# Seven block products in place of eight for one pair of weight pieces per group, in the last network's down projections

## The chip, the cores and the metric

The kernel runs on one core of a Trainium2 chip. The metric is the device time of one execution in microseconds (us), the median of several. The engines are PE (TensorE matmul), PEld (its weight loads), DVE (VectorE), ACT (ScalarE), POOL (GpSimd) and SP (SyncE, which only issues transfers here).

## The reference, cut to what matters

Two transformer blocks run one after the other on 256 tokens of width 2048, all in fp32. The change touches only the end of the second block, its feed-forward network:

```python
hn = rms_norm_2(h, norm_ffn_g)
gate, up = jnp.split(hn @ w_gate_up, 2, axis=-1)     # 2048 -> 2 x 5632
h = h + (jax.nn.silu(gate) * up) @ w_down            # 5632 -> 2048
out = rms_norm_2(h, norm_final_g)
```

## The kernel before

**Precision.** An fp32 product is made of three matmuls on rounded operands. Every operand is split in a high part and a low part (the remainder), and the kernel sums high x high, high x low and low x high. For weights ACT writes the high part (`hi`, line L552) and DVE subtracts it from the raw weights to give the low part (`lo`, L899).

**Pieces and groups.** Weights come as pieces of two k-tiles (2 x 128 rows) by 512 columns. One transfer, issued by SP, brings two pieces into one of four slots of `raw`; SP may refill a slot when both of its pieces have been split by DVE. `hi` and `lo` are rings of four pieces: ACT may write piece n when PE has used up piece n-4 (semaphore `pieces_used`). A group is the sum over some pieces into PSUM. Groups alternate between banks 0 to 3 and 4 to 7.

**The last network.** It is worked in three thirds. `f2_up0`, `f2_up1`, `f2_up2` form the hidden values of 2048, 2048 and 1536 columns, a gate group and an up group in turn, eight pieces each, 24 matmuls of 256 moving columns to a piece (L1491, L1502). After each, `f2_down0`, `f2_down1`, `f2_down2` multiply these by their part of `w_down`: four groups of 512 output columns each, of 8, 8 and 6 pieces. Here the stationary operand is a 128 x 128 tile of hidden values and the moving one is 512 columns of weights: 2 k-tiles x 2 token halves x 3 products = 12 matmuls of 512 columns to a piece (L1528 to L1530, in `piece`). Each group uses two of its four banks.

**The order on ACT and DVE.** `walk` writes it out. At piece j of a group it first calls `split` for the piece that lies AHEAD = 3 ahead (so the piece j+3 is split while PE works on j), and at the last piece it calls `evacuate` for the group. So the splits of the next group's pieces 0, 1, 2 stand in front of a group's evacuation, and that of piece 3 stands behind it (`more()` pulls a split in between steps of an evacuation). Both engines run in order.

**Evacuations.** For `f2_up` the up group's is: `work` = sums x row scale (L990), `more()`, `work` x silu (L993), ACT's copy to the high hidden values in `B` (L634), DVE's low part (L1103). For `f2_down0` and `f2_down1` (kind `tpart`): one DVE add of the two banks into `HT` (L1086). For `f2_down2` (kind `tlast`): that add, two ACT squares with sums (L608), then DVE's multiplication with the final gain (L1098). The very last group has a separate ending, in which PE takes its last four pieces twice, once for each half of the tokens (`last_pieces`), and DVE and ACT scale and store the output.

**Loops.** `f2_up1`, `f2_up2`, `f2_down0` and `f2_down1` run as hardware loops over turns (two groups to a turn); `f2_up0` and `f2_down2` are written out.

Of the kernel before, what the change touches and what calls it, by code (L numbers as in the profile page):

```python
# [25 lines left out]
P = 128  # L26
# [107 lines left out]
def ffn(add, name, n, gate, up, down, kinds, layout):  # L134

    src = n - 4
    for c, groups in enumerate((4, 4, 3)):
        first = 4 * GC * c
        add(f"{name}_up{c}", groups, ["gate", "up"], 8, ("A", "halves", src),
            [(gate[0], 0, gate[1] + first, GC), (up[0], 0, up[1] + first, GC)], peel=0 if c else groups if name == "f2" else 1)  # L140
        add(f"{name}_down{c}", 2, [kinds[c]] * 2, 2 * groups, ("B", layout, n),
            [(down, first, 0, 2 * GC), (down, first, GC, 2 * GC)], peel=2 if c == 2 else 0)
        n += groups
    return n + 4 if kinds[2] == "res_gate" else n

# [50 lines left out]
    return first or EVERY_TURN.get((seg.name, at))  # L196


class Tally:


# [35 lines left out]

def bass_two_blocks(nc, ins, out):
    SEGS, TOTAL = schedule()

    with ExitStack() as ctx:
        def sem(name):
# [5 lines left out]
        def overlay(**shapes):  # L248
# [16 lines left out]
        _, qk = overlay(pad_qk=[P, 8 * BROW], qk=[P, 16, T])  # L265
        _, xtok = overlay(pad_x=[P, 8 * BROW], xtok=[P, 2, D])
        B = sb("B", [P, KT, BROW], F32R)
        h = sb("h", [P, KT, T])
        pb_copy = sb("pb_copy", [P, MT, T])
        work = sb("work", [P, MT, T])  # L270
# [22 lines left out]
        _, win_a, win_b, win_c = overlay(g1_a=[P, KT * T], win_a=[P, MT, TM], win_b=[P, MT, TM], win_c=[P, MT, TM])  # L293
        _, cvv, cvg, cvo = overlay(g1_b=[P, KT * T], cvv=[P, MT, TV], cvg=[P, MT, TV], cvo=[P, MT, T])
        _, HT, gfin_row = overlay(silu_b=[P, MT * T], HT=[P, 2, D], gfin_row=[P, D])
        sb("arena", [P, 10368])

        ps = ctx.enter_context(nc.psum_tensor("ps", [P, 8, 512], F32))
# [23 lines left out]
        sums_written, sums_landed = sem("sums_written"), sem("sums_landed")  # L322
        skew_written, bias_landed, late_landed, stored = (
            sem("skew_written"), sem("bias_landed"), sem("late_landed"), sem("stored"))
        NTABLES = 19

        block = ctx.enter_context(nc.Block())
# [96 lines left out]
        def _(pool):  # L424
# [40 lines left out]
            small_loads(2)  # L465
            small_loads(3)

        def first_tile(seg, turn, g):
# [9 lines left out]
        def walk(eng, tallies, split, evacuate, side, each_turn, last):  # L478

            at = {"split": AHEAD}

            for seg in SEGS:
                def run(turn, t):
                    base = seg.p0 + (t or 0) * seg.per_turn

                    def split_to(end):

                        while at["split"] < end:  # L490
                            n = turn * seg.per_turn + seg.p0 + at["split"]
                            if not isinstance(n, int) or n < TOTAL:
                                split(n, base + at["split"])
                            at["split"] += 1

                    for g, kind in enumerate(seg.kinds):
                        G = turn * len(seg.kinds) + seg.g0 + g
                        for j in range(seg.pieces):
                            p = g * seg.pieces + j
                            split_to(p + 1 + AHEAD)  # L500
                            if j == seg.pieces - 1:
                                left = [MORE.get(kind, 0)]
# [6 lines left out]
                                b0 = 4 * ((seg.g0 + g + (t or 0) * len(seg.kinds)) % 2)  # L509
# [12 lines left out]
                if seg.turns > 1:  # L522
                    steady = AHEAD + MORE.get(seg.kinds[-1], 0)
                    lead = 0 if at["split"] == steady else 1
                turns_of(eng, seg, tallies, run, lead)
            last()


        @block.scalar
        def _(act):  # L530
# [12 lines left out]
            def split(n, slot):  # L543

                raw_slot = slot // 2 % RAWS
                if isinstance(n, int):
                    act.wait_ge(raw_landed[raw_slot], landed(n // 2))
                elif slot % 2 == 0 or slot < AHEAD:
                    act.wait_ge(raw_landed[raw_slot], turn_landed(n, slot))
                if not isinstance(n, int) or n >= RING:  # L550
                    act.wait_ge(pieces_used, n - RING + 1)
                act.activation(hi[:, slot % RING], raw[:, raw_slot, 2 * (slot % 2):2 * (slot % 2) + 2, :],  # L552
                               ACT.Copy).then_inc(hi_ready, 1)

            def turn_landed(n, slot):

# [317 lines left out]
            walk(act, {1: asked, 2: given, 3: ready}, split, evacuate, side, lambda quarter, turn: None, last)  # L874


        @block.vector
        def _(dve):
# [15 lines left out]
            def split(n, slot):  # L894

                dve.wait_ge(hi_ready, n + 1)
                if not isinstance(n, int) or n >= RING:
                    dve.wait_ge(pieces_used, n - RING + 1)
                dve.tensor_tensor(lo[:, slot % RING], raw[:, slot // 2 % RAWS, 2 * (slot % 2):2 * (slot % 2) + 2, :],  # L899
                                  hi[:, slot % RING], ALU.subtract).then_inc(lo_ready, 1)  # L900

            def sums_done(end):

# [526 lines left out]
            walk(dve, {0: own, 1: asked, 2: given, 3: ready}, split, evacuate, side, turn_h, last)  # L1430


        @block.tensor
        def _(pe):
# [127 lines left out]
            def side(seg, what, G):  # L1562
# [67 lines left out]
                elif isinstance(what, tuple):  # L1630
# [25 lines left out]
                    elif name == "turn_out":  # L1656
# [3 lines left out]
                                last = pe.transpose(ps[:, 6, e * T + a * P:e * T + (a + 1) * P], o_head[:, a, e * P:(e + 1) * P], ident[:, :])  # L1660
                        done.mark(last)

            def last_pieces(seg, b0):

                first = seg.pieces - RING
                for a in range(2):
                    if a == 1:
                        pe.wait_ge(residual_added, 1)
                    for j in range(first, seg.pieces):
                        n = TOTAL - seg.pieces + j  # L1670
                        if a == 0:
                            pe.wait_ge(lo_ready, n + 1)
                        for kk in range(2):
                            k = 2 * j + kk
                            Xh, Xl = (x[:, k, a * P:(a + 1) * P] for x in token_parts)
                            to = ps[:, b0 + a, :]
                            pe.matmul(to, Xh, hi[:, n % RING, kk, :], start=False, stop=False, skip_group_check=True)  # L1677
                            pe.matmul(to, Xh, lo[:, n % RING, kk, :], start=False, stop=False, skip_group_check=True)  # L1678
                            last = pe.matmul(to, Xl, hi[:, n % RING, kk, :], start=False, stop=j == seg.pieces - 1 and kk == 1, skip_group_check=True)  # L1679
                        if a == 1:  # L1680
                            last.then_inc(pieces_used, 1)
                    if a == 0:
                        last.then_inc(half_done, 1)

            for seg in SEGS:
                def run(turn, t):
                    for g, kind in enumerate(seg.kinds):
# [10 lines left out]
                        for j in range(seg.pieces - RING if at_end else seg.pieces):  # L1698
# [54 lines left out]
```

## Time and profile before

| | |
|---|---|
| median of 3 runs | 2615.46 us (2615.27 to 2615.46) |
| profiled execution, first to last instruction (span) | 2613.5 us |
| PE busy share of the span | 100% |
| DVE, ACT, POOL busy share | 62%, 45%, 1% |
| mean granted TensorE clock | 0.999 of 2.4 GHz |

The profiled execution is known by its span; the median of the runs lies 2.0 us above it, which is taken for what lies around a span. Times in the rows below are us from the start of the span unless ns is said; a matmul's busy time is longer than the distance between the starts of two, since matmuls are pipelined.

### The profile page before, as it was taken

Reading aid. Unit: us, or ns where it says so; the run is one execution under the profiler, and the core shown is the slowest. Engines: PE = TensorE matmul, PEld = TensorE weight load, DVE = VectorE, ACT = ScalarE, POOL = GpSimd, SP = SyncE. Lnnn points to the kernel's source line nnn. Section 1 sums busy time; section 2 is a strip of 40 time slices with the busy share of each in tenths; the row PEclk is TensorE's granted clock in tenths of the full one; section 3 lists DMA queues with packets and bytes.
Section 4 is the critical chain, followed back from the end, with each engine's and each line's share of the span. In section 5 each row is a group of like instructions: output and inputs, shape, how many; then the busy total and the mean of one; then the engine's idle time right before and its main releaser. Section 6 shows DMA issues by size and latency. Waiting matters only on the chain.

```text
span 2613.5 us, 50693 instructions
## 1 busy us (share of the span) xinstructions
PE 2604.7 (100%) x21336; PEld 2544.6 (97%) x21336; DVE 1614.5 (62%) x1692; ACT 1169.1 (45%) x1259; POOL 14.6 (1%) x33
## 2 busy tenths in 40 slices
PE   9999999999999999999999999999999999999998
PEld 8989999999999999999999999999999989998997
DVE  7668765555555556795676666556777655555555
ACT  5356554434443444464443333444544434443444
POOL 2000000000000000000000000000000000000000
PEclk9999999999999999999999999999999999999999
DMA  9654556565655565555555555555565555555553
GB/s 306 202 168 163 196 193 197 185 201 188 199 186 200 189 200 192 179 202 196 181 183 192 190 183 191 195 190 196 193 210 194 194 193 193 192 193 193 192 193 130
DMA packets 254438, 503.95 MB, mean 193 GB/s; under 512 B 9390, under 2 KB 11456, under 8 KB 254160
## 3 DMA queue, kind: packets, MB, share of 16 engines
q1 hardware_dynamic: 250160, 496.27, 57.2%
q10 hardware_dynamic: 3136, 4.21, 0.5%
q8 instruction: 111, 1.82, 0.3%
q0 software_dynamic: 992, 1.34, 0.2%
q14 instruction: 39, 0.32, 0.0%
HBM read 498.89 MB, written 2.89 MB: 192 GB/s over the span
## 4 chain that ended last, share of the span: by engine, by line
PE 100%; DVE 0%; ACT 0%; POOL 0%; issue 0%; DVEq 0%; POOLq 0%
PE ps L1491 49%; PE ps L1502 25%; PE ps L1528 4%; PE ps L1530 4%; PE ps L1529 4%; PE ps L1549 4%; PE ps L1558 4%; PE ps L1553 3%; PE ps L1539 1%; PE ps L1538 1%; PE ps L1536 1%; PE ps L1444 0%; PE ps L1451 0%; PE ps L1679 0%; PE ps L1678 0%; PE ps L1677 0%
## 5 line engine op out<-in xcount | busy, mean ns | idle before, releaser
L899 DVE TENSOR_TENSOR lo<-raw,hi 128x1024 fp32r<-128x1024 f32 x939 | 1142.6, 1224 | 864.5 <-ACT hi L552 850.3
L552 ACT ACTIVATE hi<-raw 128x1024 fp32r<-128x1024 f32 x939 | 990.3, 1060 | 1237.0 <-PE ps L1502 938.8
L1491 PE MATMUL ps<-A,hi 128*128 128x256 f32 x7286 | 902.8, 276 | 0.0
L1491 PEld LDWEIGHTS ps<-A,hi 128*128 128x128 f32 x7286 | 861.0, 188 | 0.3
L1491 PE MATMUL ps<-B,hi 128*128 128x256 f32 x3963 | 491.0, 276 | 0.0
L1502 PE MATMUL ps<-A,lo 128*128 128x256 f32 x3648 | 487.7, 276 | 0.0
L1491 PEld LDWEIGHTS ps<-B,hi 128*128 128x128 f32 x3963 | 468.2, 188 | 0.1
L1502 PEld LDWEIGHTS ps<-A,lo 128*128 128x128 f32 x3648 | 447.3, 188 | 0.0
L1502 PE MATMUL ps<-B,lo 128*128 128x256 f32 x1984 | 265.2, 276 | 0.0
L1502 PEld LDWEIGHTS ps<-B,lo 128*128 128x128 f32 x1984 | 243.3, 188 | 0.0
L1529 PE MATMUL ps<-lo,B 128*128 128x512 f32 x336 | 130.7, 389 | 0.0
L1528 PE MATMUL ps<-hi,B 128*128 128x512 f32 x336 | 130.7, 389 | 0.0
L1530 PE MATMUL ps<-hi,B 128*128 128x512 f32 x336 | 130.7, 389 | 0.0
L1549 PE MATMUL ps<-B,hi 128*128 128x260 f32 (+3 forms) x768 | 109.0, 284 | 0.0
L1558 PE MATMUL ps<-B,lo 128*128 128x258 f32 (+3 forms) x768 | 108.7, 284 | 0.0
L1553 PE MATMUL ps<-B,hi 128*128 128x256 f32 x768 | 104.1, 278 | 0.0
L1549 PEld LDWEIGHTS ps<-B,hi 128*128 128x128 f32 x768 | 100.0, 189 | 0.0
L1558 PEld LDWEIGHTS ps<-B,lo 128*128 128x128 f32 x768 | 98.9, 189 | 0.0
L1553 PEld LDWEIGHTS ps<-B,hi 128*128 128x128 f32 x768 | 96.3, 188 | 0.0
L1528 PEld LDWEIGHTS ps<-hi,B 128*128 128x128 f32 x336 | 63.1, 188 | 13.1
L1530 PEld LDWEIGHTS ps<-hi,B 128*128 128x128 f32 x336 | 63.1, 188 | 13.0
L1529 PEld LDWEIGHTS ps<-lo,B 128*128 128x128 f32 x336 | 63.1, 188 | 13.0
(264 smaller groups left out, 1235.0 us busy)
## 6 DMA issues: line engine op xcount, KB each, us to landing
raw<-in_w_in_dram SPq DMA_DIRECT2D x135, 1024.0 KB, 5.2
raw<-in_ffn_w_dram SPq DMA_DIRECT2D x132, 1024.0 KB, 5.1
raw<-in_w_gate_up_dram SPq DMA_DIRECT2D x88, 1024.0 KB, 5.0
raw<-in_w_down_dram SPq DMA_DIRECT2D x44, 1024.0 KB, 5.1
raw<-in_w_out_dram SPq DMA_DIRECT2D x16, 1024.0 KB, 5.1
raw<-in_pl_w_gate_dram SPq DMA_DIRECT2D x16, 1024.0 KB, 5.0
raw<-in_conv_out_w_dram SPq DMA_DIRECT2D x16, 1024.0 KB, 5.1
raw<-in_w_o_dram SPq DMA_DIRECT2D x16, 1024.0 KB, 5.0
```

Of the source, the lines that this page charges most:

```text
L552: act.activation(hi[:, slot % RING], raw[:, raw_slot, 2 * (slot % 2):2 * (slot % 2) + 2, :], ACT.Copy).then_inc(hi_ready, 1)
L899: dve.tensor_tensor(lo[:, slot % RING], raw[:, slot // 2 % RAWS, 2 * (slot % 2):2 * (slot % 2) + 2, :], hi[:, slot % RING], ALU.subtract). ...
L1491: pe.matmul(ps[:, b0 + m, 0:T], high(slot, kk, m), x, start=j == 0 and kk == 0 and part == 0, stop=False)
L1502: last = pe.matmul(ps[:, b0 + m, 0:T], low(slot, kk, m), Xh, start=False, stop=j == seg.pieces - 1 and kk == 1)
L1528: pe.matmul(to, Xh, hi[:, slot % RING, kk, :], start=first, stop=False)
L1529: pe.matmul(to, Xh, lo[:, slot % RING, kk, :], start=False, stop=False)
L1530: last = pe.matmul(to, Xl, hi[:, slot % RING, kk, :], start=False, stop=final)
L1536: pe.matmul(to, Wh, Xh, start=first and m % 2 == 0, stop=False, skip_group_check=True)
L1538: pe.matmul(to[:, a:b], Wh, Xl[:, a:b], start=False, stop=False, skip_group_check=True)
L1549: pe.matmul(ps[:, b0 + m, 0:with_lo], high(slot, kk, m), B[:, 2 * j + kk, 0:with_lo], start=first and kk == 0, stop=False, skip_group_chec ...
L1553: pe.matmul(ps[:, b0 + m, 0:T], high(slot, kk, m), B_low[:, 2 * j + kk, :], start=False, stop=False, skip_group_check=True)
L1558: last = pe.matmul(ps[:, b0 + m, 0:with_hi], low(slot, kk, m), B[:, 2 * j + kk, 0:with_hi], start=False, stop=final and kk == 1, skip_grou ...
```

## The change

For pieces 2 and 3 of every group of the three down projections but the very last group (11 pairs), the two pieces of weights and the hidden values they meet are read as 2 x 2 blocks (two k-tiles by two column halves, two token halves by two k-tiles), and the 2 x 2 block product is made with seven products of blocks and not eight, in the manner of Strassen and Winograd. `seven_products` on PE makes them: each is three matmuls of 256 columns, 42 to a pair, where 24 of 512 columns stood.

For this, POOL forms sums of weight blocks from `raw` (`block_sums`, four `tensor_tensor` of 128 x 512 elements to a pair, one of them in place in `raw`), ACT and DVE split three of these into `t_hi` and `t_lo` (128 x 1536 elements), sums of the hidden values are formed once to each third (`activation_sums`, at the up evacuation of the second turn), and `combine` adds the parts of the products that lie in two more banks into `HT`, by one ACT copy and five DVE operations, at piece 5 of the group. ACT's split of piece 2 waits for POOL, and so does DVE's of piece 3. The loops of the last network are written out.

```diff
-            ... peel=0 if c else groups if name == "f2" else 1)
+            ... peel=groups if name == "f2" else 0 if c else 1)
-            ... peel=2 if c == 2 else 0)
+            ... peel=2 if c == 2 or name == "f2" else 0)
+SEVEN_AT = 2
+SEVEN_COLS = GC // 2
+def seven_product_pairs(segs):
+    first = [x.p0 + turn * x.per_turn + g * x.pieces + SEVEN_AT
+             for x in segs if x.name.startswith("f2_down") for turn in range(2) for g in range(2)]
+    return {n: q for q, n in enumerate(first[:-1])}
...
+            def block_sums(n, q):                                    # GpSimd
+                w = raw[:, n // 2 % RAWS, :, :].rearrange("p (i e) (s c) -> p i e s c", e=2, s=2)
+                t3, t2, t4 = (t_sum[:, :, i, :] for i in range(3))
+                pool.wait_ge(raw_landed[n // 2 % RAWS], landed(n // 2))
+                if q:
+                    pool.wait_ge(t_lo_ready, q)
+                pool.tensor_tensor(t3, w[:, :, 1, 1, :], w[:, :, 0, 1, :], ALU.subtract).then_inc(t3_set, 1)
+                pool.wait_ge(t3_set, q + 1)
+                pool.tensor_tensor(w[:, :, 0, 1, :], w[:, :, 0, 1, :], w[:, :, 0, 0, :], ALU.subtract).then_inc(t1_set, 1)
+                pool.tensor_tensor(t2, t3, w[:, :, 0, 0, :], ALU.add).then_inc(t2_set, 1)
+                pool.wait_ge(t2_set, q + 1)
+                pool.tensor_tensor(t4, w[:, :, 1, 0, :], t2, ALU.subtract).then_inc(t_set, 1)
...
                             split_to(p + 1 + AHEAD)                  # walk
+                            if t is not None and j == SEVEN_AT + 3 and base + g * seg.pieces + SEVEN_AT in PAIRS:
+                                combine(PAIRS[base + g * seg.pieces + SEVEN_AT], b0, turn * len(seg.kinds) + g)
                             if j == seg.pieces - 1:
...
+                                if sums:
+                                    activation_sums(more)
...
+                if isinstance(n, int) and n in PAIRS:                # ACT, split
+                    act.wait_ge(t1_set, PAIRS[n] + 1)
                 act.activation(hi[:, slot % RING], raw[...], ACT.Copy).then_inc(hi_ready, 1)
+                if isinstance(n, int) and n - 1 in PAIRS:
+                    act.wait_ge(t_set, q + 1)
+                    act.activation(t_hi[:, :, :, :], t_sum[:, :, :, :], ACT.Copy).then_inc(t_hi_ready, 1)
...
+            def combine(q, b0, gi):                                  # ACT
+                wait(ready)
+                act.wait_ge(t_used, q + 1)
+                act.activation(work[:, 0, :], ps[:, b0 + 2, 0:SEVEN_COLS], ACT.Copy).then_inc(p1_copied, 1)
...
+                if isinstance(n, int) and n - 1 in PAIRS:            # DVE, split
+                    dve.wait_ge(t_hi_ready, PAIRS[n - 1] + 1)
+                    dve.tensor_tensor(t_lo[:, :, :, :], t_sum[:, :, :, :], t_hi[:, :, :, :], ALU.subtract).then_inc(t_lo_ready, 1)
...
+            def combine(q, b0, gi):                                  # DVE
+                x = HT[:, :, gi * GC:(gi + 1) * GC]
+                p1, v5, v7, u2 = (work[:, i, :] for i in range(4))
+                dve.wait_ge(p1_copied, q + 1)
+                step(dve.tensor_tensor(u2, p1, ps[:, b0 + 2, SEVEN_COLS:GC], ALU.add))
+                step(dve.tensor_tensor(work[:, 1:3, :], row_of(u2, 2), ps[:, b0 + 3, :].rearrange("p (s c) -> p s c", s=2), ALU.add))
+                dve.tensor_tensor(x[:, 0, :], x[:, 0, :], work[:, 0:2, :].rearrange("p s c -> p (s c)"), ALU.add)
+                x1 = x[:, 1, :].rearrange("p (s c) -> p s c", s=2)
+                step(dve.tensor_tensor(x1, x1, row_of(v7, 2), ALU.add))
+                step(dve.tensor_tensor(x[:, 1, SEVEN_COLS:GC], x[:, 1, SEVEN_COLS:GC], ps[:, b0 + 3, 0:SEVEN_COLS], ALU.add))
+            def activation_sums(more):                               # DVE: four sums of 128 x 256, one split of 128 x 1024
...
+            def seven_products(j, slot, b0, n):                      # PE
+                def product(to, start, stop, x, w_hi, w_lo):
+                    pe.matmul(to, x[0], w_hi, start=start, stop=False, skip_group_check=True)
+                    pe.matmul(to, x[0], w_lo, start=False, stop=False, skip_group_check=True)
+                    return pe.matmul(to, x[1], w_hi, start=False, stop=stop, skip_group_check=True)
...
+                pe.wait_ge(s_ready, PAIRS[n] // 4 + 1)
+                for i in range(2):
+                    k = 2 * (j + i)
+                    pe.wait_ge(lo_ready, n + i + 1)
+                    product(p16[:, 0:half], i == 0, False, tokens(0, k), *block(0, 0, i))
+                    product(z0[:, 0:half], False, False, tokens(0, k + 1), *block(1, 0, i))
+                    product(z0[:, half:GC], False, False, summed(3, i), *block(1, 1, i))
+                    product(p57[:, 0:half], i == 0, False, summed(0, i), *block(0, 1, i)).then_inc(pieces_used, 1)
+                pe.wait_ge(t_lo_ready, PAIRS[n] + 1)
+                for i in range(2):
+                    k = 2 * (j + i)
+                    product(p16[:, half:GC], False, i == 1, summed(1, i), *block_sum(1, i))
+                    product(p57[:, half:GC], False, i == 1, summed(2, i), *block_sum(0, i))
+                    last = product(z1[:, 0:half], False, False, tokens(1, k + 1), *block_sum(2, i))
+                last.then_inc(t_used, 1)
...
-                            if seg.reads[1] == "wide" or seg.reads[1] == "conv" and not two_passes(seg, g):
+                            if isinstance(n, int) and n in PAIRS:
+                                seven_products(j, slot, b0, n)
+                            elif isinstance(n, int) and n - 1 in PAIRS:
+                                pass
+                            elif seg.reads[1] == "wide" or seg.reads[1] == "conv" and not two_passes(seg, g):
```

## Rows read from the trace of the kernel before

**Rows 1.** The page: the span, and busy time of each engine

```profile
span 2613.5 us, 50693 instructions
PE 2604.7 (100%) x21336; PEld 2544.6 (97%) x21336; DVE 1614.5 (62%) x1692; ACT 1169.1 (45%) x1259; POOL 14.6 (1%) x33
```

**Rows 2.** The page: the chain that ended last, by engine

```profile
PE 100%; DVE 0%; ACT 0%; POOL 0%; issue 0%; DVEq 0%; POOLq 0%
```

**Rows 3.** Windows of f2_down1 and f2_down2: length, busy PE, PEld, DVE, ACT

```profile
2322.90:2410.00 87.10, 87.10 (x387) 72.12 (x386) 46.08 (x38) 34.77 (x33) 0.00 (x0) 1.00 0.58 193
2540.90:2606.00 65.10, 65.10 (x290) 53.88 (x288) 40.02 (x42) 30.09 (x41) 0.00 (x0) 1.00 0.37 128
```

**Rows 4.** Timeline of PE: start, duration, instruction; a piece in f2_up1, one in f2_down1

```profile
2271.13 1.98 PE L1491 MATMUL ps<-A,hi 128*128 128x256 f32 x16
2273.85 1.98 PE L1491 MATMUL ps<-A,hi 128*128 128x256 f32 x16
...
2339.48 0.39 PE L1529 MATMUL ps<-lo,B 128*128 128x512 f32 x1
2342.20 0.39 PE L1529 MATMUL ps<-lo,B 128*128 128x512 f32 x1
```

**Rows 5.** Groups by line and shape, from 2050 us: busy us, mean ns

```profile
L899 DVE TENSOR_TENSOR lo<-raw,hi 128x1024 fp32r<-128x1024 f32 x202 | 246.4, 1224 | 222.3 <-ACT hi L552 220.2 <-DVE work L990 1.0 <-DVE work L983 1.0
L552 ACT ACTIVATE hi<-raw 128x1024 fp32r<-128x1024 f32 x201 | 212.0, 1060 | 282.5 <-PE ps L1502 165.8 <-PE ps L1530 116.4
L608 ACT ACTIVATE pb_copy<-HT 128x512 f32<-128x512 f32 x6 | 3.7, 624 | 7.3 <-DVE HT L1086 7.3
L1411 DVE TENSOR_TENSOR HT<-HT,ps 128x512 f32<-128x512 f32 x1 | 0.7, 689 | 1.9 <-PE ps L1679 1.9
```

**Rows 6.** Timeline of DVE: a short operation, and what waits for it

```profile
340.63 0.42 DVE L923 TENSOR_TENSOR sumsq<-sumsq,tiny 128x256 f32<-128x256 f32 x1
341.09 1.22 DVE L899 TENSOR_TENSOR lo<-raw,hi 128x1024 fp32r<-128x1024 f32 x1
```

**Rows 7.** Timeline of DVE in f2_down2, first to second group

```profile
2555.88 1.23 DVE L899 TENSOR_TENSOR lo<-raw,hi 128x1024 fp32r<-128x1024 f32 x1 [1.49 <-ACT hi L552]
2557.45 1.22 DVE L1086 TENSOR_TENSOR HT<-HT,ps 128x1024 f32<-128x1024 f32 x1 [0.34 <-PE ps L1530]
2560.07 1.23 DVE L1098 TENSOR_TENSOR HT<-HT,gfin_row 128x1024 f32<-128x1024 f32 x1 [1.40 <-ACT pb_copy L608]
2561.22 2.36 DVE L899 TENSOR_TENSOR lo<-raw,hi 128x1024 fp32r<-128x1024 f32 x2
```

**Rows 8.** Timeline of ACT at the same boundary

```profile
2554.79 1.06 ACT L552 ACTIVATE hi<-raw 128x1024 fp32r<-128x1024 f32 x1 [1.66 <-PE ps L1530]
...
2559.95 1.99 ACT L552 ACTIVATE hi<-raw 128x1024 fp32r<-128x1024 f32 x2
```

**Rows 9.** Timeline of DVE at the start of f2_down1 and its first group's end

```profile
2324.70 1.23 DVE L899 TENSOR_TENSOR lo<-raw,hi 128x1024 fp32r<-128x1024 f32 x1 [0.19 <-DVE work L990]
2325.84 1.22 DVE L993 TENSOR_TENSOR work<-work,silu_s 128x1024 f32<-128x1024 f32 x1
2328.56 1.23 DVE L1103 TENSOR_TENSOR B<-work,B 128x1024 f32 x1 [1.51 <-ACT B L634]
2329.70 2.35 DVE L899 TENSOR_TENSOR lo<-raw,hi 128x1024 fp32r<-128x1024 f32 x2
...
2344.90 1.22 DVE L1086 TENSOR_TENSOR HT<-HT,ps 128x1024 f32<-128x1024 f32 x1 [0.34 <-PE ps L1530]
```

**Rows 10.** Groups of POOL's own work in the whole span

```profile
L428 POOL TENSOR_SCALAR_AFFINE_SELECT ident<-ident 128x128 f32<-128x128 f32 x1 | 0.3, 282 | 0.2 <-POOL ones L426 0.2
L425 POOL MEMSET ident<- 128x128 f32 x1 | 0.2, 204 | 0.3 <-POOLq L1743 0.3
L1743 POOL MEMSET const-float32-0.0<- 128x1 f32 x1 | 0.1, 93 | 0.3 <-issue 0.3
```

**Rows 11.** The page: weight transfers, KB each, us from issue to landing

```profile
raw<-in_w_down_dram SPq DMA_DIRECT2D x44, 1024.0 KB, 5.1
```

More of the change, by code:

```diff
@@ L139, in ffn @@
         add(f"{name}_up{c}", groups, ["gate", "up"], 8, ("A", "halves", src),
-            [(gate[0], 0, gate[1] + first, GC), (up[0], 0, up[1] + first, GC)], peel=0 if c else groups if name == "f2" else 1)
+            [(gate[0], 0, gate[1] + first, GC), (up[0], 0, up[1] + first, GC)], peel=groups if name == "f2" else 0 if c else 1)
         add(f"{name}_down{c}", 2, [kinds[c]] * 2, 2 * groups, ("B", layout, n),
-            [(down, first, 0, 2 * GC), (down, first, GC, 2 * GC)], peel=2 if c == 2 else 0)
+            [(down, first, 0, 2 * GC), (down, first, GC, 2 * GC)], peel=2 if c == 2 or name == "f2" else 0)
         n += groups
@@ L239, in bass_two_blocks @@
     SEGS, TOTAL = schedule()
+    PAIRS = seven_product_pairs(SEGS)
     with ExitStack() as ctx:
@@ L267, in bass_two_blocks @@
         B = sb("B", [P, KT, BROW], F32R)
+        s_form, t_sum = overlay(s_form=([P, 2, 4, 2, P], F32R), t_sum=[P, 2, 3, SEVEN_COLS])
         h = sb("h", [P, KT, T])
@@ L295, in bass_two_blocks @@
         _, HT, gfin_row = overlay(silu_b=[P, MT * T], HT=[P, 2, D], gfin_row=[P, D])
+        _, t_hi, t_lo = overlay(gfin_end=[P, MT * T + 3 * D], t_hi=([P, 2, 3, SEVEN_COLS], F32R), t_lo=([P, 2, 3, SEVEN_COLS], F32R))
         sb("arena", [P, 10368])
@@ L324, in bass_two_blocks @@
             sem("skew_written"), sem("bias_landed"), sem("late_landed"), sem("stored"))
+        t1_set, t_set, t_hi_ready, t_lo_ready, t_used = (
+            sem("first_block_sums_set"), sem("block_sums_set"), sem("block_sums_hi"), sem("block_sums_lo"), sem("block_sums_used"))
+        t2_set, t3_set = sem("third_block_sum_set"), sem("second_block_sum_set")
+        s_ready, p1_copied = sem("activation_sums_ready"), sem("first_product_copied")
         NTABLES = 19
@@ L466, in _ @@
             small_loads(3)
+            def block_sums(n, q):
[10 more added lines that the diff above has]
+                pool.tensor_tensor(t4, w[:, :, 1, 0, :], t2, ALU.subtract).then_inc(t_set, 1)
+            pool.wait_ge(h_turned, 16)
+            for n, q in PAIRS.items():
+                block_sums(n, q)
         def first_tile(seg, turn, g):
@@ L476, in first_tile, with walk @@
             return (turn * len(seg.kinds) + g) * MT
-        def walk(eng, tallies, split, evacuate, side, each_turn, last):
+        def walk(eng, tallies, split, evacuate, side, each_turn, combine, activation_sums, last):
             at = {"split": AHEAD}
@@ L500, in run @@
                             split_to(p + 1 + AHEAD)
+                            b0 = 4 * ((seg.g0 + g + (t or 0) * len(seg.kinds)) % 2)
+                            if t is not None and j == SEVEN_AT + 3 and base + g * seg.pieces + SEVEN_AT in PAIRS:
+                                combine(PAIRS[base + g * seg.pieces + SEVEN_AT], b0, turn * len(seg.kinds) + g)
                             if j == seg.pieces - 1:
-                                left = [MORE.get(kind, 0)]
+                                sums = seg.name.startswith("f2_up") and kind == "up" and t == SEVEN_AT // 2
+                                left = [MORE.get(kind, 0) + sums]
                                 def more():
@@ L508, in run @@
                                 end = turn * seg.per_turn + seg.p0 + p + 1
-                                b0 = 4 * ((seg.g0 + g + (t or 0) * len(seg.kinds)) % 2)
                                 evacuate(kind, G, end, b0, turn * len(seg.kinds) + g, first_tile(seg, turn, g), more,
                                          token_parts if seg.name.startswith("f2") else B_parts)
+                                if sums:
+                                    activation_sums(more)
                                 assert left[0] == 0, (kind, left)
@@ L551, in split @@
                     act.wait_ge(pieces_used, n - RING + 1)
+                if isinstance(n, int) and n in PAIRS:
+                    act.wait_ge(t1_set, PAIRS[n] + 1)
                 act.activation(hi[:, slot % RING], raw[:, raw_slot, 2 * (slot % 2):2 * (slot % 2) + 2, :],
                                ACT.Copy).then_inc(hi_ready, 1)
+                if isinstance(n, int) and n - 1 in PAIRS:
+                    q = PAIRS[n - 1]
+                    act.wait_ge(t_set, q + 1)
+                    if q:
+                        act.wait_ge(t_used, q)
+                    act.activation(t_hi[:, :, :, :], t_sum[:, :, :, :], ACT.Copy).then_inc(t_hi_ready, 1)
[4 more added lines that the diff above has]
+            def activation_sums(more):
+                more()
+                asked.skip()
+                wait(asked)
+                given.mark(act.activation(s_form[:, 0], pb_copy[:, :, :].rearrange("p f (i c) -> p f i c", i=2), ACT.Copy))
             def turn_landed(n, slot):
@@ L872, in last @@
                         act.dma_start(out[0, a * P:(a + 1) * P, c:e], HT[:, a, c:e]).then_inc(stored, 16)
-            walk(act, {1: asked, 2: given, 3: ready}, split, evacuate, side, lambda quarter, turn: None, last)
+            walk(act, {1: asked, 2: given, 3: ready}, split, evacuate, side, lambda quarter, turn: None, combine, activation_sums, last)
         @block.vector
@@ L898, in split, with activation_sums @@
                     dve.wait_ge(pieces_used, n - RING + 1)
+                if isinstance(n, int) and n - 1 in PAIRS:
+                    dve.wait_ge(t_set, PAIRS[n - 1] + 1)
                 dve.tensor_tensor(lo[:, slot % RING], raw[:, slot // 2 % RAWS, 2 * (slot % 2):2 * (slot % 2) + 2, :],
                                   hi[:, slot % RING], ALU.subtract).then_inc(lo_ready, 1)
+                if isinstance(n, int) and n - 1 in PAIRS:
+                    dve.wait_ge(t_hi_ready, PAIRS[n - 1] + 1)
[10 more added lines that the diff above has]
+                step(dve.tensor_tensor(x[:, 1, SEVEN_COLS:GC], x[:, 1, SEVEN_COLS:GC], ps[:, b0 + 3, 0:SEVEN_COLS], ALU.add))
+            def activation_sums(more):
+                x = work[:, :, :].rearrange("p (i e) (a c) -> p i e a c", e=2, a=2)
+                s1, s2, s3, s4 = (pb_copy[:, f, :].rearrange("p (i c) -> p i c", i=2) for f in range(4))
+                dve.tensor_tensor(s1, x[:, :, 0, 1, :], x[:, :, 1, 1, :], ALU.add)
+                step(dve.tensor_tensor(s3, x[:, :, 0, 0, :], x[:, :, 0, 1, :], ALU.subtract))
+                step(dve.tensor_tensor(s2, s1, x[:, :, 0, 0, :], ALU.subtract))
+                hand(dve.tensor_tensor(s4, x[:, :, 1, 0, :], s2, ALU.subtract))
+                more()
+                given.skip()
+                wait(given)
+                dve.tensor_tensor(s_form[:, 1], pb_copy[:, :, :].rearrange("p f (i c) -> p f i c", i=2), s_form[:, 0],
+                                  ALU.subtract).then_inc(s_ready, 1)
             def sums_done(end):
@@ L1428, in last @@
                         dve.tensor_scalar(HT[:, a, c:e], HT[:, a, c:e], r, None, ALU.mult).then_inc(left_scaled, 1)
-            walk(dve, {0: own, 1: asked, 2: given, 3: ready}, split, evacuate, side, turn_h, last)
+            walk(dve, {0: own, 1: asked, 2: given, 3: ready}, split, evacuate, side, turn_h, combine, activation_sums, last)
         @block.tensor
@@ L1661, in side, with tokens, summed, block @@
                         done.mark(last)
+            def seven_products(j, slot, b0, n):
+                Xh, Xl = token_parts
+                half = SEVEN_COLS
+                def product(to, start, stop, x, w_hi, w_lo):
+                    pe.matmul(to, x[0], w_hi, start=start, stop=False, skip_group_check=True)
+                    pe.matmul(to, x[0], w_lo, start=False, stop=False, skip_group_check=True)
+                    return pe.matmul(to, x[1], w_hi, start=False, stop=stop, skip_group_check=True)
+                def tokens(a, k):
+                    return Xh[:, k, a * P:(a + 1) * P], Xl[:, k, a * P:(a + 1) * P]
+                def summed(f, i):
+                    return s_form[:, 0, f, i, :], s_form[:, 1, f, i, :]
+                def block(kk, s, i):
+                    at = (slot + i) % RING
+                    return hi[:, at, kk, s * half:(s + 1) * half], lo[:, at, kk, s * half:(s + 1) * half]
+                def block_sum(f, i):
+                    return t_hi[:, i, f, :], t_lo[:, i, f, :]
+                z0, z1, p16, p57 = (ps[:, b0 + i, :] for i in range(4))
+                pe.wait_ge(s_ready, PAIRS[n] // 4 + 1)
[13 more added lines that the diff above has]
+                last.then_inc(t_used, 1)
             def last_pieces(seg, b0):
```

## Prediction

> **What bounds the kernel now.** I read the page's busy times first. PE is busy for 2604.7 of 2613.5 us, DVE and ACT for little more than half of it, and GpSimd does next to nothing after the start [rows 1]. The chain that ended last says the same: all of it is PE, and waiting has no share [rows 2]. So time falls only where PE gets less to do, and only as long as no other engine becomes late. Next come the windows of the down projections. `f2_down1` takes 87.1 us for 384 matmuls, `f2_down2` 65.1 for 288, with no PE idle time, and DVE is already busy for 53% and 61% of them [rows 3]. The timeline of PE gives the price of a matmul: two pieces of `f2_up1` start 2.72 us apart, which is 24 matmuls of 256 columns, so 113.3 ns each; in `f2_down1` the 12th matmul of 512 columns after another starts 2.72 us later, so 226.7 ns each [rows 4]. There is no fixed part: half the columns cost half.
>
> **PE's part.** A pair of pieces was 24 x 226.7 ns = 5.44 us and becomes 42 x 113.3 ns = 4.76 us. That is 0.68 us less, and over 11 pairs 7.48 us, if every product finds its operands ready. The stationary tiles stay 128 x 128, and a weight load to each 256 columns is what `f2_up1` does now at 113.3 ns.
>
> **Loops written out.** The looped `f2_down1` and the written-out `f2_down2` have the same 226.7 ns to a matmul (87.1 / 384 and 65.1 / 288, within the window's edge) [rows 3]. I take nothing for it; a gain is excluded, since PE has no idle time to give back, and a loss, from more code to be fetched, is left to the upper bound.
>
> **Prices on ACT and DVE.** DVE takes 0.42 us for 256 elements in a row, 0.69 for 512 and 1.22 for 1024, ACT 0.62 for 512 and 1.06 for 1024; an operation that waits for the one before it starts 0.04 us after its end [rows 5, 6]. Along these lines 1536 elements are 1.75 us on DVE (`t_lo`) and 1.50 on ACT (`t_hi`). `combine` is 0.42 + 3 x 0.69 + 0.42 + steps = 3.0 us on DVE, and 0.40 on ACT. The activation sums are four operations of 0.42, one of 1.22 and an ACT copy of 1.06, once to each third.
>
> **Groups of eight pieces (8 of the 11 pairs).** `combine` stands at piece 5, behind the split of the next group's piece 0, 2.7 us into piece 5. It ends 5.7 us after that piece's start. The split queued behind it ends at 6.9, and PE wants that piece 10.9 us after piece 5's start: 4 us to spare. By the group's end DVE has caught up, and the add into `HT` starts some 0.3 us behind the group's end as now [rows 9]. The low half of piece 3 and `t_lo` are then ready 2.6 and 4.4 us into the next group, and wanted at 5.44 + 1.36 = 6.8 and 8.16 us. No stall.
>
> **First groups.** At the start of a third's down projection `t_lo` (1.75 us) is put in front of the silu product [rows 9]. The low half of piece 4, now ready at 2330.9 (the first of the two splits that start at 2329.70), moves to 2332.6; PE wants it 5.44 + 4.76 us after the group's start of 2322.9 [rows 3], at 2333.1. It holds by 0.5 us. The activation sums delay the same chain by about 2 us at another group, where no piece is shortened: piece 4 then has 0.9 us left. Both are hidden, with little cover.
>
> **Groups of six pieces (`f2_down2`).** Here piece 5 is the last one. `combine` comes right in front of the group's own add, and with this kind of group ACT's squares and DVE's gain stand between that add and the split of the next group's piece 3. Now: DVE ends the split at 2557.1, the add starts at 2557.45, the gain at 2560.07, the split of piece 3 at 2561.22, ending about 2562.4 [rows 7]; ACT's high half of piece 3 is done at 2561.0 [rows 8]. With `combine` the add starts at 2560.1, 2.66 us later, and all of this moves with it. The group began at 2540.9 + 6 x 2.72 = 2557.2, so the low half of piece 3 comes 2.66 us late at 2565.1, and PE wants it at 2557.2 + 6.80 = 2564.0: a stall of 1.1 us. `t_hi` ends at 2565.1, `t_lo` at 2566.85, and PE wants that one 1.36 us after 2565.1: 0.4 us more. That is 1.5 us each in the second and third group. The last group has no pair, but its last four pieces are taken one token half at a time, so that it wants piece 3 at the same 6.8 us: 1.1 us. Together 4.1 us given back.
>
> **GpSimd.** No row shows it at a two-operand operation. Its memset of 128 elements takes 0.20 us, its select of 128 elements 0.28, a one-element memset 0.09 [rows 10]. Four times the elements at the memset's slope is 0.53 us; at the select's slope, doubled for two operands, 1.6 us. I take 1.2, near the upper end since the select is the nearer row: 4.8 us to a pair. The transfer of a pair's weights lands 5.1 us after its issue [rows 11], which DVE's split of seven pieces earlier releases, so in groups of eight there are about 10 us until ACT wants the first two sums (2.4 us). Between the second and third group of `f2_down2` GpSimd starts only after `t_lo` and needs 2.4 of the 4.8 us there are. Alone, it costs PE nothing. What it may cost is DVE's time, if the two engines can't work on SBUF at once. The trace of before can't show that, since GpSimd is idle whenever DVE matters. The bounds: nothing, or each sum pushes DVE's queue by its own duration where the cover is thin. In front of the third group of `f2_down2` DVE has 7.4 us from the end of `t_lo` to `combine` and five splits of 1.15 to do in them, so 1.65 free, and 4 x 1.2 - 1.65 = 3.2 us are pushed on; at its first group three sums fall on 1.5 us of idle time and 0.5 of cover, 1.6 us; at the two other first groups one sum on the 0.5 of cover, 0.7 each: 6.2 us in all. I take 2.4, below the middle, since the sums can also fall into DVE's gaps.
>
> The Trainium skill's page "SBUF — State Buffer", section "SBUF: two separate sides", speaks for the upper bound: an operation of VectorE with two SBUF inputs and one of GpSimd that reads SBUF exclude each other for their whole length. No run here shows it yet. By that rule the sum would end at 2618.2, without it at 2612.1.
>
> **The sum.** The span of 2613.5 becomes 2613.5 - 7.5 + 4.1 + 2.4 = 2612.5; 2.0 us lie around it by the median, so 2614.5 us. A difference of under 0.2% (5.2 us) can hardly be told from none here, and this is one.
>
> **The rivals.**
> 1. *Nearly all of the saving arrives*: stalls of 2.2 us or less in all, as when `combine` overlaps what I put in a row, or GpSimd disturbs nothing and the squares' chain has more cover. 7.48 - 2.2 is just faster by 0.2%; the full saving is 2608.0. For it: PE is the only bound, DVE has 40% free. Against it: rows 7 and 8 show a chain in which every link waits for the last. 20%.
> 2. *My forecast*, part of the saving lost in `f2_down2` and to DVE's sharing: 2610.2 to 2620.7, likeliest 2614.5. This includes that `t_lo` or a GpSimd sum is late by one or two us in single groups. 63%.
> 3. *GpSimd's sums hold DVE up*, slower than before. With x for one sum, the blocked time is 4x - 1.65 at the third group, 3x - 2 at the first group of `f2_down2`, x - 0.5 at the two others: 9x - 4.65. It must pass 8.6 us to be slower by 0.2%, which is at x = 1.47; at the 1.6 of the upper bound the time is 2615.5 - 7.5 + 4.1 + 9.8 = 2621.9. Longer still, DVE's 15.2 us (eight splits of 1.15, 1.75, 3.0, 1.22) and GpSimd's 4x no longer fit into the 21.1 us of a group of eight, and every group stalls. For it: DVE is the next engine in line. Against: it needs the long end of x and no luck in the order. 17%, with code fetching in it.
>
> The Trainium skill's "GPSIMD Engine Reference", section "Performance versus the Vector engine", has 4497 ns for 2048 elements of two fp32 operands; by an estimate from that page 512 elements are about 1.12 us, below the 1.47 at which this rival decides.
>
> So faster 20%, same 63%, slower 17%. The range takes the full saving at its lower end (2608) and the third rival's price at its upper (2622).
>
> **What would show it.** Right: `f2_down0` and `f2_down1` each 2.7 us shorter, `f2_down2` 2.0 us less PE work but 2 us or more of PE idle time at its second to last groups, released by DVE's `lo` or `t_lo`; the add into `HT` there 2.7 us later after its group's end. Wrong: PE's waits elsewhere, in the first groups above all; `lo` splits longer than 1.23 us or late while GpSimd works; sums of over 1.5 us; 256 columns at more than 113.3 ns in `seven_products`.

## The result, and the profile after

The changed kernel takes 2620.25 us (median of 17 runs), the kernel before 2615.46: a ratio of 1.0018 with a 95% interval of 1.0011 to 1.0025. It is slower by 4.8 us. That is just under the 0.2% that the prediction took for the limit of what can be told, but the interval lies clear of 1. The forecast was 2614.5 us, so the number was 5.7 us too low and the sign was wrong; the time lies inside the range.

The page of the changed kernel, its span and busy times, then its chain (answering [rows 1, 2]):

```profile
span 2618.2 us, 50645 instructions
PE 2602.6 (99%) x21534; PEld 2551.0 (97%) x21534; DVE 1692.0 (65%) x1773; ACT 1188.9 (45%) x1284; POOL 97.5 (4%) x77
```

```profile
PE 98%; DVE 1%; POOL 0%; ACT 0%; issue 0%; DVEq 0%; ACTq 0%; POOLq 0%
```

PE has less busy time but is no longer 100% of the chain: 1% is DVE now. The windows of `f2_down0`, `f2_down1` and `f2_down2` say where (length; busy PE, PEld, DVE, ACT, POOL; granted clock), answering [rows 3]:

```profile
2061.40:2147.40 86.00, 85.38 (x458) 73.84 (x458) 68.23 (x63) 41.29 (x41) 23.83 (x13) 1.00 0.57 192
2322.00:2407.20 85.20, 85.20 (x458) 73.79 (x457) 71.37 (x62) 41.18 (x41) 20.98 (x12) 1.00 0.56 194
2538.20:2610.70 72.50, 66.39 (x343) 56.90 (x342) 60.19 (x60) 34.10 (x47) 17.64 (x8) 0.98 0.33 116
```

The first two became 1.1 and 1.9 us shorter, where 2.7 had been expected; the third became 7.4 us longer. There PE is idle for 6 us, and its mean clock is not full. The waits of PE in the changed kernel (who waited for whom; total, times, longest) are all for DVE's low parts (the entry for `ident` is the start of the program, as before):

```profile
PE ps L1761 <- DVE lo L962: 5.2, 2, 3.3
PE ps L1536 <- POOL ident L447: 1.7, 1, 1.7
PE ps L1809 <- DVE lo L962: 0.8, 1, 0.8
PE ps L1620 <- DVE lo L962: 0.6, 1, 0.6
```

PE's timeline at the longest of them, in the pair of the third group of `f2_down2`, with the window from there on (same columns as above):

```profile
2579.33 0.28 PE L1763 MATMUL ps<-hi,s_form 128*128 128x256 f32 x1
2582.87 0.41 PE L1761 MATMUL ps<-hi,B 128*128 128x256 f32 x1 [3.27 <-DVE lo L962]
2583.09 0.40 PE L1762 MATMUL ps<-lo,B 128*128 128x256 f32 x1
2583.29 0.42 PE L1763 MATMUL ps<-hi,B 128*128 128x256 f32 x1
```

```profile
2582.90:2586.60 3.70, 3.70 (x18) 3.70 (x19) 3.70 (x3) 3.56 (x4) 0.00 (x0) 0.54 0.65 221
2586.60:2595.00 8.40, 8.40 (x45) 7.18 (x44) 5.23 (x7) 1.51 (x3) 0.00 (x0) 1.00 0.08 29
```

Matmuls of 256 columns start 213 ns apart there and not 113 to 120: the granted clock is 0.54 of full, its lower level (1.2 GHz) nearly all through, after PE had waited. It is back at 1.00 in the next window, PE having worked for 3.7 us without a pause. About 17 matmuls started some 100 ns later than at full clock, which makes the 1.7 us that are counted for the clock below.

What made DVE late is seen when its timeline and GpSimd's are laid side by side, between the second and third group of `f2_down2`. DVE:

```profile
2563.07 1.76 DVE L966 TENSOR_TENSOR t_lo<-t_sum,t_hi 128x1536 fp32r<-128x1536 f32 x1
2564.75 10.21 DVE L962 TENSOR_TENSOR lo<-raw,hi 128x1024 fp32r<-128x1024 f32 x5
2574.89 0.41 DVE L973 TENSOR_TENSOR work<-work,ps 128x256 f32<-128x256 f32 x1
...
2577.84 1.22 DVE L1178 TENSOR_TENSOR HT<-HT,ps 128x1024 f32<-128x1024 f32 x1
2580.46 1.22 DVE L1190 TENSOR_TENSOR HT<-HT,gfin_row 128x1024 f32<-128x1024 f32 x1 [1.40 <-ACT pb_copy L669]
2581.60 1.22 DVE L962 TENSOR_TENSOR lo<-raw,hi 128x1024 fp32r<-128x1024 f32 x1
```

GpSimd:

```profile
2564.98 2.17 POOL L494 TENSOR_TENSOR t_sum<-raw 128x512 f32<-128x512 f32 x1 [13.07 <-DVE t_lo L966]
2567.23 2.15 POOL L496 TENSOR_TENSOR raw<-raw 128x512 f32<-128x512 f32 x1
2569.34 2.29 POOL L497 TENSOR_TENSOR t_sum<-t_sum,raw 128x512 f32<-128x512 f32 x1
2571.71 2.17 POOL L499 TENSOR_TENSOR t_sum<-raw,t_sum 128x512 f32<-128x512 f32 x1
```

Five splits take 10.2 us, 2.04 each, where before each took 1.22, and about 1.15 in a row [rows 5, 7]; the four sums take 2.2 us each. `combine` starts at 2574.89, behind all five; the add, the gain and the split of piece 3 follow in the order of [rows 7], and PE gets piece 3 at 2582.8.

Where a single split and a single sum meet, in `f2_down0`, the one that started first keeps its time and the other is longer by the wait for it. First a sum that meets no split, 1.31 us, then a sum that starts 0.22 us after a split:

```profile
2096.91 1.31 POOL L497 TENSOR_TENSOR t_sum<-t_sum,raw 128x512 f32<-128x512 f32 x1
2098.08 1.23 DVE L962 TENSOR_TENSOR lo<-raw,hi 128x1024 fp32r<-128x1024 f32 x1 [3.66 <-ACT hi L596]
2098.30 2.17 POOL L499 TENSOR_TENSOR t_sum<-raw,t_sum 128x512 f32<-128x512 f32 x1
```

The split took its usual 1.23 us. So the two operations take turns and don't slow each other throughout. The other engines hardly wait for the sums themselves: ACT and DVE 3.3 us in all, only at the very first pair.

### The profile page after: what moved, and what is told of

It is laid out like the page before. It is cut to its first block, busy times and chain, and to the rows that moved or that the text cites. A ratio compares the mean times of both kernels' runs of the same rounds, so it can differ in the third digit from the quotient of the medians.

```text
span 2618.2 us, 50645 instructions
## 1 busy us (share of the span) xinstructions
PE 2602.6 (99%) x21534; PEld 2551.0 (97%) x21534; DVE 1692.0 (65%) x1773; ACT 1188.9 (45%) x1284; POOL 97.5 (4%) x77
## 4 chain that ended last, share of the span: by engine, by line
PE 98%; DVE 1%; POOL 0%; ACT 0%; issue 0%; DVEq 0%; ACTq 0%; POOLq 0%
PE ps L1583 49%; PE ps L1594 24%; PE ps L1641 4%; PE ps L1650 4%; PE ps L1645 3%; PE ps L1620 3%; PE ps L1622 3%; PE ps L1621 3%; PE ps L1761 1%; PE ps L1763 1%; PE ps L1762 1%; PE ps L1631 1%; PE ps L1630 1%; PE ps L1628 1%; DVE lo L962 0%
## 5 line engine op out<-in xcount | busy, mean ns | idle before, releaser
L962 DVE TENSOR_TENSOR lo<-raw,hi 128x1024 fp32r<-128x1024 f32 x939 | 1164.0, 1249 | 797.1 <-ACT hi L596 783.6
L494 POOL TENSOR_TENSOR t_sum<-raw 128x512 f32<-128x512 f32 x11 | 19.4, 1763 | 2460.5 <-DVE HT L1218 2026.3
L1620 PE MATMUL ps<-hi,B 128*128 128x512 f32 x248 | 97.0, 391 | 0.6 <-DVE lo L962 0.6
L1622 PE MATMUL ps<-hi,B 128*128 128x512 f32 x248 | 96.6, 390 | 0.0
L1621 PE MATMUL ps<-lo,B 128*128 128x512 f32 x248 | 96.5, 389 | 0.0
L695 ACT ACTIVATE B<-work 128x1024 f32 (+1 forms) x26 | 27.6, 1063 | 70.9 <-DVE work L1085 63.0
L1620 PEld LDWEIGHTS ps<-hi,B 128*128 128x128 f32 x248 | 46.6, 188 | 10.2 <-issue 0.8
```

What stands on the lines that cost most here:

```text
L695: given.mark(act.activation(some((A_parts if kind == "cb" else to_b)[0], k, 4, 0, T), work[:, :, :], ACT.Copy))
L1620: pe.matmul(to, Xh, hi[:, slot % RING, kk, :], start=first, stop=False)
L1621: pe.matmul(to, Xh, lo[:, slot % RING, kk, :], start=False, stop=False)
L1622: last = pe.matmul(to, Xl, hi[:, slot % RING, kk, :], start=False, stop=final)
```

## The experiments

Times are medians, each beside 2615.4 to 2615.5 us for the kernel before in the same runs. Two theories stood against each other: A, GpSimd's sums hold DVE up wherever DVE works on two SBUF operands; B, `combine` stands in the wrong place in DVE's order, and GpSimd is innocent.

**Small sums** (2614.38 us). The sums run over 4 columns of each block instead of 256, so the output is that of other weights.

```diff
+                few = slice(0, 4)
-                pool.tensor_tensor(t3, w[:, :, 1, 1, :], w[:, :, 0, 1, :], ALU.subtract)...
+                pool.tensor_tensor(t3[:, :, few], w[:, :, 1, 1, few], w[:, :, 0, 1, few], ALU.subtract)...
...
```

> GpSimd's four sums per pair work on 4 columns of each block instead of 256 (after one clearing of the sums' buffer); every wait and everything else stays as in the changed kernel, so that the down projections' values are those of other weights. Theory A (GpSimd's long operations hold up VectorE's splits, and by that the third group of f2_down2 and its clock): the splits of low parts all go back to 1.23 us, the stalls fall from 2.6 to 1.5 us in the second group of f2_down2, from 3.4 plus 1.7 of slow clock to 1.5 in the third, and the 0.8 us at the first group of f2_down0 vanish: 2614.7 us. Theory B (only the order matters, combine in front of the group's add): within 1 us of 2620.2.

5.9 us came back. PE's waits, the window of `f2_down2` and, from the timeline, the start of the second group's pair and of the piece behind it in this kernel:

```profile
PE ps L1765 <- DVE lo L966: 1.5, 2, 0.8
PE ps L1813 <- DVE lo L966: 0.8, 1, 0.8
```

```profile
2537.20:2604.50 67.30, 64.86 (x343) 55.25 (x342) 52.61 (x60) 34.00 (x47) 5.93 (x8) 1.00 0.35 124
```

```profile
2558.45 0.28 PE L1765 MATMUL ps<-hi,B 128*128 128x256 f32 x1
...
2564.72 0.40 PE L1624 MATMUL ps<-hi,B 128*128 128x512 f32 x1
```

No slow clock is left, and no wait in `f2_down0` or `f2_down1`. The pairs of the second and third group take 6.26 and 6.27 us from their first matmul to the next piece's, against 4.92 where nothing waits: 1.35 us of stall in each. So theory A is needed for 5.9 us, and theory B for what stays.

**`combine` one piece earlier** (2617.22 us, single runs 2616.93 to 2618.19).

```diff
-  if t is not None and j == SEVEN_AT + 3 and base + ... in PAIRS:
+  if t is not None and j == SEVEN_AT + 2 and base + ... in PAIRS:
```

> combine stands one piece earlier (at piece 4 of the group), all else as in the changed kernel. Theory B (order): the add into HT of f2_down2 comes 2.7 us sooner, the 1.1 us of the last group vanish, and most of the 2.6 and 5.1 us of the second and third group: about 2613 us. Theory A (VectorE and GpSimd are short of time together between two groups, wherever combine stands): the 1.1 us vanish, of the others only one to two us: 2616 to 2617.5.

Only 3.0 us came back, in theory A's range. DVE's timeline in front of the third group:

```profile
2565.04 7.94 DVE L962 TENSOR_TENSOR lo<-raw,hi 128x1024 fp32r<-128x1024 f32 x4
2572.90 0.41 DVE L973 TENSOR_TENSOR work<-work,ps 128x256 f32<-128x256 f32 x1
...
2575.85 1.22 DVE L962 TENSOR_TENSOR lo<-raw,hi 128x1024 fp32r<-128x1024 f32 x1
2576.99 1.21 DVE L1178 TENSOR_TENSOR HT<-HT,ps 128x1024 f32<-128x1024 f32 x1
```

Counted from the first of the splits behind `t_lo`, the add starts 11.95 us later, where it was 13.09 in the changed kernel: 1.1 us sooner and not 2.7, as the four splits in front of `combine` still take 2 us each. The wait of the last group is gone. The slow clock now fell on the second group's pair instead, after a wait of 2.0 us.

**Both edits** (2610.48 us; output as with the small sums).

> Both edits, the small sums and combine at piece 4 (values as in the first run). If order and GpSimd's hold on VectorE are all that stalls PE, no stall is left, and what remains of the loss is the rate in the pairs (0.16 us above 42 x 113.3 ns, 11 times): 2615.5 - 7.5 + 1.8 = 2609.8. If something else of the change costs time (code written out, waits of PE itself), it stays above 2611.

No PE wait is left in the last network, and the window of `f2_down2` is all PE:

```profile
2537.10:2600.70 63.60, 63.60 (x343) 55.13 (x342) 52.58 (x60) 34.82 (x47) 5.94 (x8) 1.00 0.39 132
```

The two causes together explain all waiting. What is left between 2615.4 - 7.5 = 2607.9 and 2610.5 is 1.8 us for the rate of the matmuls within the pairs (below) and small rests.

**No pairs in `f2_down2`** (2612.49 us, ratio 0.9989, interval 0.998 to 0.9998).

```diff
-             for x in segs if x.name.startswith("f2_down") for turn in range(2) for g in range(2)]
-    return {n: q for q, n in enumerate(first[:-1])}
+             for x in segs if x.name in ("f2_down0", "f2_down1") for turn in range(2) for g in range(2)]
+    return {n: q for q, n in enumerate(first)}
```

> The pairs of f2_down2 are taken out; the eight pairs of f2_down0 and f2_down1 stay. Theories A and B both say that nearly all of the loss is in f2_down2: 8 x (0.68 - 0.16) = 4.2 us saved, about 1 us lost at the first groups: 2612.3 us, faster than both. If written-out code or GpSimd costs time everywhere, 2615 or more.

As expected: three pairs cost 7.8 us more than they save, the other eight save 3.

**The loops alone** (2615.38 us): the kernel before with only the two changes of `peel`.

> The kernel before with the last network's loops written out, as in the change, and nothing else of it. All theories so far: no difference, 2615.4 us. If fetching the longer code costs, 2616 to 2618, with PE waits that no semaphore ends.

No difference (ratio 0.9999, 0.999 to 1.0009), and no wait.

**GpSimd alone** (2616.0 us, single runs 2615.73 to 2617.17, ratio 1.0003, 0.9994 to 1.0012). The kernel before, with sums that nobody needs.

```diff
+            pool.wait_ge(h_turned, 16)
+            for i in range(120):
+                if i:
+                    pool.wait_ge(idle_sum, i)
+                pool.tensor_tensor(h[:, 4:6, :], h[:, 0:2, :], h[:, 2:4, :], ALU.add).then_inc(idle_sum, 1)
```

> The kernel before; once the residual has been turned, GpSimd adds 128 x 512 elements of a dead buffer to others, 120 times in a row, for which nobody waits. Theory A (GpSimd and VectorE operations with two SBUF operands exclude each other): a sum takes about 1.3 us where VectorE is idle and about 2.2 where it is not, VectorE's splits go up to 2.3 us, its operations with a PSUM operand stay at 1.22, and PE stalls at the ends of the up groups: 2617 to 2625 us. If both only share bandwidth: splits and PSUM operations alike get some longer. If the change's loss came from its waits alone: splits stay at 1.23 and the time at 2615.4.

Groups of DVE, then of POOL, in this kernel from 2056 to 2320 us (busy us, mean ns):

```profile
L905 DVE TENSOR_TENSOR lo<-raw,hi 128x1024 fp32r<-128x1024 f32 x98 | 184.3, 1909 | 46.9 <-ACT hi L558 45.8 <-DVE work L996 0.4 <-DVE work L989 0.4
L999 DVE TENSOR_TENSOR work<-work,silu_s 128x1024 f32<-128x1024 f32 x4 | 9.2, 2309 | 0.0
L1092 DVE TENSOR_TENSOR HT<-HT,ps 128x1024 f32<-128x1024 f32 x4 | 4.9, 1215 | 0.3 <-PE ps L1536 0.3
L996 DVE TENSOR_TENSOR work<-ps,r_row 128x1024 f32<-128x1024 f32 x4 | 4.8, 1211 | 0.0
```

```profile
L472 POOL TENSOR_TENSOR h<-h 128x512 f32<-128x512 f32 x120 | 242.7, 2023 | 2035.9 <-DVE HT L1132 2026.6
```

This is the hold by itself. Operations with two SBUF operands go from 1.22 us to 1.9 and 2.3 on average; those of the same size with one PSUM operand stay at 1.21. Bandwidth shared by all would have lengthened both. The time rose by only half a microsecond, which lies within the interval, and not to the expected 2617 to 2625: groups of eight pieces have cover enough. So a lengthened split is not yet a loss; it is one where a late split is wanted at once.

**Eight of the pairs, `combine` early** (2611.66 us, ratio 0.9986, interval 0.9977 to 0.9995).

```diff
-    return {n: q for q, n in enumerate(first[:-1])}
+    return {n: q for q, n in enumerate(first[1:9])}
...
-                pe.wait_ge(s_ready, PAIRS[n] // 4 + 1)
+                pe.wait_ge(s_ready, (PAIRS[n] + 1) // 4 + 1)
```

The move of `combine` is the one above; the second edit shown keeps each pair's wait at its own third, as the pairs are now counted from the second.

> The changed kernel with eight of the pairs: without the first group of f2_down0 and without the second and third of f2_down2, and with combine at piece 4. If these three pairs are all that costs more than it saves: 2615.4 - 8 x 0.52 + 0.4 for small rests = 2611.6 us, below both kernels. If the first group's stall belongs to the first pair wherever it stands, 2612.4.

As expected, and faster than both kernels: left out are the very first pair and those of the second and third group of `f2_down2`. No run has these eight pairs with `combine` in its first place, so the share of that move is not shown.

**Operands moved by 64 bytes.** The pairs took 4.92 us even where nothing waited, and not 4.76. PE's timeline in the changed kernel shows which matmuls:

```profile
2089.05 0.28 PE L1761 MATMUL ps<-hi,B 128*128 128x256 f32 x1
2089.16 0.28 PE L1762 MATMUL ps<-lo,B 128*128 128x256 f32 x1
2089.28 0.28 PE L1763 MATMUL ps<-hi,B 128*128 128x256 f32 x1
2089.40 0.28 PE L1761 MATMUL ps<-hi,B 128*128 128x256 f32 x1
...
2089.76 0.28 PE L1761 MATMUL ps<-hi,s_form 128*128 128x256 f32 x1
...
2090.44 0.28 PE L1761 MATMUL ps<-hi,B 128*128 128x256 f32 x1
...
2093.97 0.40 PE L1620 MATMUL ps<-hi,B 128*128 128x512 f32 x1
```

Of the first 24 matmuls, those with hidden values (`B`) as the stationary tile are 120 ns apart, six with activation sums (`s_form`) from 2089.76 to 2090.44 are 113. The last 18, on the block sums, are 118 apart on average. Two kernels move one operand each, from the kernel with eight of the pairs.

```diff
-TOKEN_AT = 16
+TOKEN_AT = 0
```

> As the kernel with eight of the pairs, with the hidden values 64 bytes lower in each row of B. In the pairs 12 of 42 matmuls start 120 ns behind the one before and not 113.3, all of them with a stationary tile from B. If that is by where the tile lies against the moving weights within 128 bytes: these go to 113.3 ns, 0.08 us less to a pair, 0.6 us in all. If it is by anything else: no change.

2613.19 us (single runs 2612.96 to 2618.39), slower by 1.5 and not faster by 0.6. In its first pair the matmuls with `B` do start 113 ns apart, as the theory has it, and that pair takes 4.85 us; but the matmuls of 512 columns, which use the same tiles, lose more:

```profile
2080.58 0.39 PE L1620 MATMUL ps<-hi,B 128*128 128x512 f32 x1
...
2083.32 0.39 PE L1620 MATMUL ps<-hi,B 128*128 128x512 f32 x1
```

2.74 us to a piece, not the 2.72 of [rows 4], and there are 72 such pieces.

```diff
-        _, t_hi, t_lo = overlay(gfin_end=[P, MT * T + 3 * D], t_hi=...
+        _, t_hi, t_lo = overlay(gfin_end=[P, MT * T + 3 * D + 16], t_hi=...
```

> As the kernel with eight of the pairs, hidden values where they were, and the split block sums (the moving operand of the last 18 matmuls of a pair) 64 bytes higher in each row. These 18 start 118 ns apart on average now. If what counts is whether the stationary tile and the moving operand lie at the same place within 128 bytes: the twelve with activation sums as stationary tiles go to 113.3 ns and the six with hidden values stay or rise to 120; 0.05 us less to a pair, 2611.2 us. If it is by anything else: 2611.7.

2611.5 us (ratio 0.9985, 0.9976 to 0.9994): the pair goes from 4.92 to 4.89, not by the expected 0.05. Where the operands lie changes the rate, but the simple rule about 128 bytes is refuted in part: in the kernel with the hidden values moved, four of the eight pairs ran at 117.8 ns where the rule gives 113.3. What the rule is stays open.

## Why the prediction was wrong

- **What bounds the kernel**: right. Every microsecond is one of PE's, working, waiting or at the slow clock.
- **PE's part, 7.48 us**: too large. The price of 113.3 ns came from `f2_up1` with its operands in other places; in the pairs it is 117 ns on average, 4.92 us to a pair. The saving is 11 x 0.52 = 5.7 us. The term is off by 1.8 us.
- **Loops written out, nothing**: right, by the run with the loops alone.
- **Groups of eight pieces, no stall**: right. The add and the splits there had cover enough even at 2 us to a split.
- **Groups of six pieces, 4.1 us**: right in place and nearly in size. With small sums the two pairs stalled 1.35 us each (forecast 1.5) and the last group 1.1 (forecast 1.1), 3.8 us; with `combine` earlier as well, the time is 3.9 us shorter.
- **GpSimd, 2.4 us**: the step that failed most. The mechanism was named, but the value taken was too low. The run with small sums gives 5.9 us, of which 1.7 are the slow clock, so 4.2 are waits: the term is off by 1.8 us, as much as PE's, and by 3.5 with the clock that hung on its longest wait. The upper bound of 6.2 us was too high by 2.0. The estimate of 1.2 us to a sum was good (1.3 alone), but "the sums can also fall into DVE's gaps" was not: behind `t_lo` DVE has a queue of splits, so each sum met one and each made the other wait. The Trainium skill's page "SBUF — State Buffer", section "SBUF: two separate sides", has a GpSimd operation that reads SBUF and a VectorE operation with two SBUF inputs exclude each other for an operation's whole length. The trace agrees (1.9 to 2.3 us against 1.21 with a PSUM operand), and the time of 2618.2 by that rule (by chance the same number as the span above) would have been nearer to the 2620.25 measured, in part by luck: its 6.2 us are more than the 4.2 of waits, which made up for some of the rate and the clock that it lacks too.
- **First groups**: the cover of 0.5 us was rightly called thin. In `f2_down0` piece 4 came 0.8 us late (by the starts of the matmuls; the list of waits, from the end of one, has 0.6), behind the splits of 2 us. In `f2_down1` 0.15 us were lost.
- **Not in the sum at all**: the clock. After a wait of 3.3 us PE ran for 3.7 us at 1.2 GHz, 1.7 us lost. The prediction counted waits only at their own length.

Together, in spans: 2613.5 - 7.5 + 1.8 (rate) + 4.2 (GpSimd) + 3.9 (order) + 1.7 (clock) = 2617.6; 2618.2 was measured. Of the rest of 0.6, 0.4 stands in the kernel with both edits too, in which PE waits nowhere (a span of 2608.2 against 2613.5 - 7.5 + 1.8 = 2607.8); what it is was not taken apart. By its time the result still lies in the second rival's range, up to 2620.7. By its cause it is a milder form of the third, though not by its long sums: at 1.3 us to a sum its own formula gives 7.1 us and not 4.2.

## What to carry to other kernels

Before work is put on GpSimd, look at what VectorE does in the same microseconds: with two SBUF operands on both, their times nearly add (five splits of 1.15 us and four sums of 1.3 took 10.2 here), so count them as one queue and take no discount for gaps unless the timeline shows one at that place. Then price a stall where an order has no cover, and allow for the slow clock, which stood behind some of the waits here; the same sums in groups with 4 us of cover cost nothing, and leaving out the three pairs without cover, with `combine` a piece earlier, turned 0.18% slower into 0.14% faster. A matmul's price read in one stage need not hold in another where its operands lie elsewhere.

## What the runs showed of the hardware that had not been expected

- Matmuls of 256 columns with a 128 x 128 stationary tile started 113.3, 117.8 or 120 ns apart in one and the same stage, depending on where in a row the two operands lay; a shift of 64 bytes changed it both ways. With 512 columns, twelve took 2.74 us in place of 2.72.
- A PE wait of 1.98 us in the changed kernel (second group) left the clock at full speed; one of 1.99 us with `combine` one piece earlier was followed by 1.2 GHz (granted clock 0.51 over the 3.5 us from 2563.9), as was one of 3.27 us in the changed kernel. What decides was not tried.
